# Bias rows of blocks 1 and 2 spread by GpSimd instead of by DMA, and the last parameters fetched behind the last expert weights

## What is computed

```python
def moe_ffn(xn, w_router, b_router, w_gate, b_gate, w_up, b_up, w_down, b_down):
    ...                                   # top 4 of 32 experts for each token
    def expert_block(args):
        toks, e = args
        h = x_pad[toks]
        gate = jnp.minimum(h @ w_gate[e] + b_gate[e], SWIGLU_LIMIT)
        up = jnp.clip(h @ w_up[e] + b_up[e], -SWIGLU_LIMIT, SWIGLU_LIMIT)
        glu = gate * jax.nn.sigmoid(SWIGLU_ALPHA * gate)
        return ((up + 1.0) * glu) @ w_down[e] + b_down[e]
    ...                                   # weighted sum over each token's experts
h = h + moe_ffn(rms_norm(h, norm_ffn_g), ...)
return rms_norm(h, norm_final_g)
```

## Time and profile before

| | us |
|---|---|
| median of 3 runs | 1583.55 |
| lowest, highest run | 1581.59, 1583.69 |
| the profiled execution | 1588.09 |
| its span, first to last instruction | 1586.4 |

### The profile page before, as it was taken

The page is one execution under the profiler, slowest core; times in us unless marked ns, Lnnn a source line. Parts: engine busy times, 40 slices in busy tenths (PEclk is TensorE's granted clock), DMA queues, the critical chain, the costliest instruction groups (busy, mean ns, idle before and its releaser), DMA issues.

```text
span 1586.4 us, 29423 instructions
## 1 busy us (share of the span) xinstructions
PE 1534.9 (97%) x10453; PEld 1267.6 (80%) x10453; DVE 1323.5 (83%) x1458; ACT 1086.6 (68%) x1316; POOL 598.5 (38%) x371
## 2 busy tenths in 40 slices
PE   7999987889999999999999999999999999999997
PEld 6877767886888788878888888888888888888884
DVE  4256455554689999999999999999999999999996
ACT  4245431102477888877888888788888788888874
POOL 7000312101030224235555456545435555444553
PEclk9999998999999999999999999999999999999999
DMA  7321110001589999999999999999999999999994
GB/s 245 90 67 41 40 42 2 4 4 68 199 320 371 403 367 366 404 359 398 398 387 386 377 395 393 393 387 385 374 384 393 392 390 392 388 369 392 395 386 164
DMA packets 81275, 464.33 MB, mean 293 GB/s; under 512 B 11643, under 2 KB 12855, under 8 KB 33073
## 3 DMA queue, kind: packets, MB, share of 16 engines
q1 hardware_dynamic: 71424, 438.68, 70.2%
q0 software_dynamic: 9104, 24.52, 6.8%
q10 hardware_dynamic: 672, 0.07, 0.0%
HBM read 449.16 MB, written 23.13 MB: 298 GB/s over the span
## 4 chain that ended last, share of the span: by engine, by line
PE 83%; DVE 11%; DMA 3%; issue 2%; ACT 1%; POOL 0%; SPq 0%; POOLq 0%; ACTq 0%; DVEq 0%
PE banks L380 68%; DVE expert_w_lo L320 6%; PE banks L1839 5%; PE banks L2102 1%; PE banks L1932 1%; PE banks L2099 1%; DMA expert_w_raw<-in_moe_w_up_dram 1%; PE banks L1916 1%; PE banks L2037 1%; DMA gate_bias_rows<-in_moe_b_gate_dram 1%; PE banks L2084 1%; PE banks L2111 1%; ACT expert_w_hi L315 0%; DMA y_sums<-y_block,scatter_rows 0%; PE banks L2362 0%
## 5 line engine op out<-in xcount | busy, mean ns | idle before, releaser
L320 DVE TENSOR_TENSOR expert_w_lo<-expert_w_raw,expert_w_hi 128x1024 fp32r<-128x1024 f32 x764 | 908.2, 1252 | 31.1 <-ACT expert_w_hi L315 30.7
L315 ACT ACTIVATE expert_w_hi<-expert_w_raw 128x1024 fp32r<-128x1024 f32 x764 | 750.2, 1056 | 32.5 <-DMA expert_w_raw<-in_moe_w_down_dram 24.4
L380 PE MATMUL banks<-expert_w_hi,x_block_T_hi 128*128 128x512 f32 x1008 | 395.8, 393 | 2.1 <-DVE expert_w_lo L320 2.0
L380 PE MATMUL banks<-expert_w_lo,x_block_T_hi 128*128 128x512 f32 x1008 | 392.8, 390 | 0.0
L380 PE MATMUL banks<-expert_w_hi,x_block_T_lo 128*128 128x512 f32 x1008 | 392.5, 389 | 0.0
L742 POOL COPY scatter_gates<-slot_gate 128x1 f32 x26 | 225.5, 8674 | 249.3 <-DMA y_sums<-y_block,scatter_rows 249.3
L380 PEld LDWEIGHTS banks<-expert_w_hi,x_block_T_hi 128*128 128x128 f32 x1008 | 189.4, 188 | 43.1 <-DVE expert_w_lo L320 3.9
L380 PEld LDWEIGHTS banks<-expert_w_lo,x_block_T_hi 128*128 128x128 f32 x1008 | 189.2, 188 | 39.6
L380 PEld LDWEIGHTS banks<-expert_w_hi,x_block_T_lo 128*128 128x128 f32 x1008 | 189.3, 188 | 38.2
L380 PE MATMUL banks<-expert_w_hi,h_block_T_hi 128*128 128x512 f32 x528 | 209.4, 397 | 4.8 <-DVE expert_w_lo L320 4.2
L380 PE MATMUL banks<-expert_w_lo,h_block_T_hi 128*128 128x512 f32 x528 | 206.1, 390 | 0.0
(11 more groups left out here) (397 smaller groups left out, 1975.8 us busy)
## 6 DMA issues: line engine op xcount, KB each, us to landing
expert_w_raw<-in_moe_w_up_dram SPq DMA_DIRECT2D x128, 1024.0 KB, 7.9
expert_w_raw<-in_moe_w_down_dram SPq DMA_DIRECT2D x128, 1024.0 KB, 9.7
expert_w_raw<-in_moe_w_gate_dram SPq DMA_DIRECT2D x126, 1024.0 KB, 10.1
w_raw<-in_w_in_dram SPq DMA_DIRECT2D x24, 512.0 KB, 3.7
residual<-in_x_dram SPq DMA_DIRECT2D x8, 512.0 KB, 5.1
w_raw<-in_w_out_dram SPq DMA_DIRECT2D x8, 512.0 KB, 3.3
staged_raw<-in_moe_w_gate_dram SPq DMA_DIRECT2D x2, 1024.0 KB, 6.0
y_sums<-residual SPq DMA_DIRECT2D x4, 512.0 KB, 7.4
```

The lines of the kernel that those rows point to most:

```text
L315: act.activation(self.hi[:, k % self.nhl, 0:width], self.raw[:, slot, 0:width], ACT.Copy)\
L320: dve.tensor_tensor(self.lo[:, k % self.nhl, 0:width], self.raw[:, (k - self.staged) % self.nraw, 0:width], self.hi[:, k % self.nhl, 0:wid ...
L380: last = pe.matmul(o, lhs, rhs, start=start and t == 0, stop=stop and t == 2, skip_group_check=preset)
```

## The change

For blocks 1 and 2 the two bias rows come as one row of 4 KB and are spread by GpSimd, as from block 3 on. GpSimd spreads block 1's gate bias right behind the two gathers that come ahead of the block loop, and its up bias and those of block 2 at the places that `block_pool` has for them. ACT's `gate_bias` and `up_bias` of blocks 1 and 2 wait for `bias_spread` instead of for the transfer. The transfers of `norm_final_g` and `down_bias_rows` move on SP from between the loads of blocks 1 and 2 to behind the last weight load.

```diff
             def bias_load(i, rows, name, e, landed):
-                if isinstance(i, int):
-                    sp.dma_start(rows[:, :], bias_rows(name, e)).then_inc(landed, 16)
-                else:
-                    sp.dma_start(rows[0:1, :], bias_of(name, e)).then_inc(landed, 16)
+                sp.dma_start(rows[0:1, :], bias_of(name, e)).then_inc(landed, 16)
...
             block_loads(1, 1, 0)
-            sp.dma_start(g_fin[:, :], t_in["norm_final_g"].partition_broadcast(P)).then_inc(S("late_params_in"), 16)
-            for q in range(4):
-                sp.dma_start(bd4[32 * q:32 * q + 32, :], t_in["moe_b_down"][0]).then_inc(S("late_params_in"), 16)
             block_loads(2, 2, 1)
...
             loads(nb, 0, wd_v, expert(last_blk))
+            sp.dma_start(g_fin[:, :], t_in["norm_final_g"].partition_broadcast(P)).then_inc(S("late_params_in"), 16)
+            for q in range(4):
+                sp.dma_start(bd4[32 * q:32 * q + 32, :], t_in["moe_b_down"][0]).then_inc(S("late_params_in"), 16)
...
-                pool.wait_ge(S("bias_spread"), i * 2 + which - 5)
+                pool.wait_ge(S("bias_spread"), i * 2 + which - 1)
...
             def block_pool(i, e):
                 at = i * 4 - 4 * LOOP0
-                spread = not (isinstance(i, int) and i < 3)
-                if spread:
+                if not (isinstance(i, int) and i == 1):
                     spread_bias(i, 0)
                 pool.wait_ge(S("xT_ps"), i + 2)
                 keep_gates(i, e, at)
                 gather(i + 1, at + 1)
-                if spread:
-                    spread_bias(i, 1)
+                spread_bias(i, 1)
...
+            spread_bias(1, 0)
             pool.wait_ge(S("gates0_in"), 16)
             ch.link(pool.tensor_copy(slot_gate[:, 0:1], gate0[:, 0:1]))
...
         def gate_bias(act, i):
-            if isinstance(i, int) and i < 3:
-                act.wait_ge(S("gate_bias_in"), i * 16 + 16)
+            if isinstance(i, int) and i == 0:
+                act.wait_ge(S("gate_bias_in"), 16)
             else:
-                act.wait_ge(S("bias_spread"), i * 2 - 5)
+                act.wait_ge(S("bias_spread"), i * 2 - 1)
```

More of the change, by code:

```diff
@@ L849, in up_bias @@
         def up_bias(act, i):
-            if isinstance(i, int) and i < 3:
-                act.wait_ge(S("up_bias_in"), i * 16 + 16)
+            if isinstance(i, int) and i == 0:
+                act.wait_ge(S("up_bias_in"), 16)
             else:
-                act.wait_ge(S("bias_spread"), i * 2 - 4)
+                act.wait_ge(S("bias_spread"), i * 2)
             if not (isinstance(i, int) and i == 0):
```

## The result

The changed kernel takes 1591.15 us (median of 7 runs, 1587.89 to 1595.10); the kernel before, on the same chip and between them, 1582.86 us (7 runs, 1575.78 to 1583.69). The ratio is 1.0062 with a 95% interval of 1.0043 to 1.0080: slower by some 8 to 10 us, where 3.7 were forecast. It lies just above the range (1591.0), and the interval excludes the forecast.

The account below looks back on a forecast made before the run. Mostly VectorE was taken to bound 476.44 to 618.65, then TensorE to the end of the block loop. First spread +4.8, spreads +3.5 and lighter load -4.6 gave +3.7 us: 1583.55 to 1587.2, range 1579.5 to 1591.0.

Parts of the forecast that it names:

- Late parameters: End of the program: moved behind the last weights, they land by about 1558, ahead of TensorE's read at 1568.56; no cost.
- The lighter load: VectorE between 476.44 and 618.65: less DMA load removes waits for weights and block 3's spread; 4.6 us gained.
- What spreads cost VectorE: Blocks 1 to 3: spreads beside VectorE's chunks slow it, 1.0 for block 1's up spread, 2.0, 0.5; sum 3.5 us.
- The first spread: Block 1's gate bias: a 6.12 us code load delays ACT, and VectorE enters the bound stretch 4.8 us late.
- The sum: At 618.65: +4.8 + 3.5 - 4.6 = +3.7 us, which stays to the end.
- The load waits for the transfers: Rival, block 1's first spread: GpSimd's load begins only when the gathers have landed; +5.4 more, 1592.6; chance 0.09.
- The hidden load: Rival, block 1's first spread: load overlaps the gathers ahead, ACT does not wait; -0.1, 1583.5; chance 0.16.
- the relief that wins: Rival, blocks 1 to 3: load hidden and spreads cost VectorE little; -4.0, 1579.6, faster; chance 0.12.

Follow-up runs that it names:

- e8: Kernel before with late parameters moved behind the last weights, iota ahead of the gate map and a 32-column scratch spread right behind it; ratio 0.9994.
- e11: Changed kernel with block 1's gate-bias spread between the two gathers, tokens ahead of it and gates behind; ratio 1.0041.
- e12: Kernel before with only the late parameters moved behind the last expert weights, measured again in more rounds; ratio 0.9987.
- b2: Kernel before, unchanged, traced a second time; stretch from first expert matmul to last token transposes 1058.3 us.
- e5: Changed kernel with the late parameters put back between the weights of blocks 1 and 2, leaving the spreads alone; ratio 1.0062.
- e1: Kernel before with only the late parameters moved behind the last weights; ratio 0.9974.
- e9: Changed kernel with block 1's bias rows fetched whole by DMA again, spreads from block 2 on; ratio 0.9998.
- e10: Changed kernel with 30 extra matmuls on TensorE in the pause behind block 0's last up chunk; ratio 1.0054.
- e4: Changed kernel with block 1's gate-bias spread ahead of the two gathers; ratio 1.0005.
- e3: Changed kernel with block 1's gate-bias spread behind the wait for the gathered gate values and their copy; 1593.55 us, one run.
- e2: Changed kernel with one more spread, of 32 columns, among GpSimd's first constants at 30 us; ratio 1.0074.
- e7: Changed kernel with block 1's gate-bias spread right behind the gate map, ahead of the memsets of `x_block`, and the iota ahead of the map; ratio 1.0016.

## Why the prediction was wrong, step by step

**Late parameters: right in the trace of the changed kernel, but an end that can bind was overlooked.** From the last token transposes to the end of the span are 74.6 us before and 74.5 after. But in e8, e11 and e12, where the parameters come late too, it is 75.2, 75.9 and 75.9, and there the chain that ended last runs through another code load of GpSimd. It is that of the comparison at line 800 (`onehot_last`), the first instruction behind the spreads that needs other code. It stands in the trace of before as well, ahead of the last adding of rows to memory:

```profile
1554.44 3.46 POOL L800 TENSOR_SCALAR onehot_last<-iota_tokens,last_row 128x512 fp32r<-128x512 f32 x1 [8.30 <-issue]
```

```profile
L800 POOLq MODIFY_POOL_CONFIG  x2: 11/11/11, 1546.4 to 1546.4; - x2
```

In e12 the chain has it as follows:

```profile
1538.81 10.79 issue
1549.60 2.92 POOL onehot_last L800
```

From configuration to comparison it takes 7.8 to 8.1 us in the three traces with the parameters in their old place (before, b2, e5), and 8.3 to 10.9 in the eleven with them at the end. So the move may lengthen this load, and so the end by up to 1.3 us; no run tests that by itself. It could be part of why e12's median gains less than its stretch.

**The lighter load: right in size by the first trace, half of it by the second; -4.6 forecast.** From block 2 to block 10 it is -4.2 against the first trace of before and -2.4 against b2; e1 and e12 give -4.4 against the first trace and -2.6 against b2. VectorE's idle time of the earlier trace rows is gone. The cause is less simple than told: either part of the change alone removes most of it (e1 and e5), since the late first spread in block 3 is among what goes, and the pause in block 1 lets the weights catch up.

**What spreads cost VectorE: right per row, wrong for the sum; +3.5 forecast.** Where a spread meets chunks they take 1 us more: three in 4.46 us in block 1 (3 x 1.135 = 3.4 without), and in block 2 the seven of this row of VectorE's timeline in the changed kernel:

```profile
499.60 9.00 DVE L320 TENSOR_TENSOR expert_w_lo<-expert_w_raw,expert_w_hi 128x1024 fp32r<-128x1024 f32 x7
```

Before, the same seven took 8.04. But only the one in block 1 is seen to be paid for, inside the 10.4 us. Blocks 2 and 3 pay 0.3 to 0.4 us (e9 against e12, net of two lighter transfers) where I had 2.5. VectorE's idle time is used up as forecast (39.03 of 39.17 us busy), but the step from there to each microsecond of a spread counting failed. What takes it up is not shown.

**The first spread: the term that was mis-sized; +4.8 forecast, and 1.0 for the up spread behind it.** The place, the order and the chain (ScalarE, three chunks, `x_block_T_lo`, TensorE) are those forecast. The size failed twice. First, I took 6.12 us for the load from the row of line 750, and it was 10.65. I had read that line as the only one with a configuration; the load of 8.30 us at line 800, above, stood in the same trace and would have shown that the time varies. Measured from the first expert matmul, the gate bias starts 15.32 us in before and 24.03 after, 8.7 late instead of 6.04: 6.04 and 4.53 more from the load, less 1.37 because GpSimd came to the spread 1.14 earlier than in the trace of before and 0.23 for the queue did not arise, less 0.49 for a spread of 1.30 instead of 1.79. `h_block` ends 26.80 us in before and 35.25 after: VectorE is 8.45 late where 5.8 were forecast. Second, the halved clock behind TensorE's pause, which the forecast had at nothing: from `h_block` to block 2's transposes another 1.98 us go, 2.6 for the clock less 0.6 of VectorE's delay that was taken up. 8.45 + 1.98 = 10.4. e10 shows the second by itself and e4 and e9 both by their absence.

**The sum.** 5.8 + 2.5 - 4.6 = 3.7 was forecast; the rows give 10.4 + 0.3 - 4.4 = 6.3, and 6.1 was measured. Against b2 it is 7.5, and the runs say 6.8 to 12.7 (1.0043 to 1.0080). The traces don't account for all of the median; a longer end, as in e11 and e12, could be a part of the rest, which no run shows.

**The rivals.** "The load waits for the transfers" (0.09, 1592.6) was nearest in time. By it the spread starts some 6.1 us after the gate values land (465.35 in the changed kernel): 471.5, and it was 470.64. But e3 speaks against its mechanism, since there the load took 8.3 us with the gathers landed. The hidden load, and with it the relief that wins, fell with the first row. I gave the high side too little: the bound of that term stood in the text, the range left it out.

The rule of the Trainium skill, "GPSIMD Engine Reference", section 2.1 Instruction dispatch (about 6 us for the first call of freshly loaded code), holds for the place: the cost follows the first call. Its figure agrees with six loads here (5.6, 5.6, 5.8, 6.1, 6.1, 6.3) and roughly with four more (6.6, 7.0, 7.1, and 7.1 for e2's iota), and not with the five behind a gather (10.6 to 11.1), with e3's 8.3 or with those at the end (7.8 to 10.9).

**Open.** What makes a load 10.6 to 11.1 us long when an indirect gather has been issued just ahead of it (after, e2, e5, e10, e11), 8.3 in e3, and 5.6 to 7.1 for the other spreads. A gather just ahead is not the only thing that does it: at the end, more than 20 us behind the last indirect transfer's issue, the load for the comparison took 7.8 to 10.9. The number of gathers is out (e11). Full DMA engines alone are out too: the 6.1 of the kernel before fell in a stretch with a DMA share of 1.00. Whether GpSimd's code still works on the gather when the load is asked for could not be seen in any row.

## What to carry to other kernels

The first call of a GpSimd routine is a load with a place of its own: look for the configuration instruction in the order, put it where GpSimd is idle and nobody waits (here the five right behind a gather were the longest), and count it again after each instruction of the other code set. A price that one row shows holds for that row's surroundings: look for the same event on every line of the trace (here 6.1 and 8.3 us), take the range (5.6 to 11.1 over all runs), and ask which pause it makes on TensorE, because here one of 7.7 us was paid again with 2.6 us at half the clock. Two parts of a change that relieve the same wait don't add up, so run each alone before one is credited with the gain.

## What the hardware showed that I had not expected

- The clock falls behind a pause and not behind each: after 1.4 us without work (e4) the granted clock stayed 1.00; after 3.8 us (e7), 4.9 (e11) and 7.7 us (the changed kernel) it was 0.50 for some 2 to 5 us. In e7 it fell only after TensorE had already restarted at 474.54, as its stretches show:

```profile
474.50:476.00 1.50, 1.46 (x9) 0.82 1.09 426
476.00:478.00 2.00, 2.00 (x6) 0.50 0.94 389
478.00:480.00 2.00, 2.00 (x8) 0.78 0.78 278
480.00:482.00 2.00, 2.00 (x11) 1.00 0.54 122
```

- GpSimd's code sets displace each other: an iota behind a spread waited 7.08 us, and the next spread 11.1 us again (e2); for a comparison (tensor_scalar) behind the last spreads the load took 7.8 to 10.9 us in every trace. Copies, memsets, affine selects and indirect gathers behind a spread ran at once.
- 30 matmuls whose results nobody reads kept the clock up and made the kernel a little faster (1.0054 against 1.0062, the intervals overlap), which only says how little TensorE's clock mattered while VectorE was as late.
